# Experts in fixed order with an overflow loop, their first weights loaded early, and the second block's parameters loaded behind the loop

## The reference

```python
scores = jax.nn.sigmoid((hf @ router_w).astype(jnp.float32))
...
_, idx = lax.top_k(jnp.where(emask, sel, -jnp.inf), TOP_K)      # 6 of 64 experts
wts = wts / jnp.sum(wts, axis=-1, keepdims=True) * ROUTED_SCALE
routed = routed_experts(hf, idx, wts.astype(h.dtype), w_gate, w_up, w_down)
shared = swiglu(hf, sw_gate, sw_up, sw_down)
return (routed + shared).reshape(B, T, D)
```

## Time and profile before

| | us |
|---|---|
| median of 3 runs (lowest, highest) | 1790.48 (1787.78, 1791.04) |
| the profiled execution | 1788.62 |
| its span in the trace | 1786.8 |
| PE busy | 1494.7 (84%) |
| DVE busy | 671.1 (38%) |
| ACT busy | 363.8 (20%) |
| DMA moved | 345.25 MB, 193 GB/s mean |

### The profile page before, as it was taken

How to read it: one execution, slowest core, us unless ns; L and a number is a source line. 1 busy time by engine, 2 the same in 40 slices (tenths; PEclk the granted TensorE clock), 3 DMA queues, 4 the chain that set the end, 5 groups by cost and what they waited for, 6 DMA issues and landing times.

```text
span 1786.8 us, 18426 instructions
## 1 busy us (share of the span) xinstructions
PE 1494.7 (84%) x6948; PEld 918.7 (51%) x6948; DVE 671.1 (38%) x1200; ACT 363.8 (20%) x612; POOL 34.4 (2%) x20
## 2 busy tenths in 40 slices
PE   5884974789987899999999999569978777589996
PEld 2342441666754444444444444256656435389974
DVE  1101437533446322222222222353255523366752
ACT  0010212000001122122222222124331111244442
POOL 0000032000000000000000000000000000000000
PEclk9797985899987899999999999769958886789998
DMA  7543160022204699999999999554220221135541
GB/s 275 176 151 108 66 191 0 1 95 95 95 9 166 246 405 401 403 404 401 419 407 408 408 410 404 129 146 148 86 84 1 94 94 48 47 123 176 174 165 71
DMA packets 107278, 345.25 MB, mean 193 GB/s; under 512 B 12551, under 2 KB 38570, under 8 KB 80732
## 3 DMA queue, kind: packets, MB, share of 16 engines
q1 hardware_dynamic: 94072, 325.38, 47.7%
q10 hardware_dynamic: 8500, 15.72, 3.3%
q0 software_dynamic: 4656, 3.44, 0.8%
HBM read 339.50 MB, written 1.05 MB: 191 GB/s over the span
## 4 chain that ended last, share of the span: by engine, by line
PE 60%; DMA 13%; DVE 13%; another core or an unknown queue 4%; issue 3%; SPq 2%; ACT 2%; POOL 1%; ACTq 1%; DVEq 0%; PEldq 0%; POOLq 0%
PE bank L1136 12%; DMA gu_odd<-in_exp_w_up 9%; PE bank L1508 9%; PE bank L1155 5%; PE bank L1157 5%; PE bank L1156 5%; PE bank L1167 2%; PE bank L1528 2%; PE bank L1321 2%; PE bank L1465 2%; PE bank L1580 1%; DMA ring<-in_ada_b 1%; PE bank L1466 1%; PE bank L1483 1%
## 5 line engine op out<-in xcount | busy, mean ns | idle before, releaser
L1136 PE MATMUL bank<-ring,xT 128*128 128x512 f32 (+3 forms) x480 | 199.9, 572 | 18.5 <-DMA ring<-in_w_in 12.9
L1136 PEld LDWEIGHTS bank<-ring,xT 128*128 128x128 f32 x480 | 93.1, 210 | 116.2 <-issue 94.3
L1528 PE MATMUL bank<-dn,tmp 128*64 128x512 f32 x544 | 124.2, 598 | 0.0
L1155 PE MATMUL bank<-mod,w_high 128*128 128x256 f32 x352 | 101.6, 289 | 11.4 <-DVE xT L2680 5.3
L2346 DVE TENSOR_TENSOR xT<-bank,mod 128x512 fp32r<-128x512 f32 x68 | 47.0, 692 | 159.9 <-ACT mod L941 159.9
L1136 PE MATMUL bank<-ring,silu_c 128*128 128x512 f32 x192 | 91.9, 623 | 18.2 <-DMA ring<-in_ada_b 17.7
L2335 DVE SCALAR_TENSOR_TENSOR tmp<-silu_c,rc,bank 128x256 f32<-128x256 f32 x34 | 23.3, 686 | 213.7 <-ACT silu_c L928 213.7
L1156 PE MATMUL bank<-xT,w_high 128*128 128x256 f32 x352 | 99.9, 284 | 0.0
L1157 PE MATMUL bank<-mod,ring 128*128 128x256 f32 x352 | 99.5, 283 | 0.0
L1167 PE MATMUL bank<-c_ident,xn 128*128 128x128 f32 x120 | 27.7, 409 | 76.0 <-DVEq L2370 50.3
L2669 DVE TENSOR_TENSOR ring<-ring,w_high 128x1024 fp32r<-128x1024 f32 x66 | 77.6, 1220 | 26.6 <-ACT w_high L1078 24.6
(11 more groups left out here) (557 smaller groups left out, 2496.6 us busy)
## 6 DMA issues: line engine op xcount, KB each, us to landing
dn<-in_exp_w_down SPq DMA_DIRECT2D x68, 1024.0 KB, 8.0
ring<-in_exp_w_gate SPq DMA_DIRECT2D x34, 1024.0 KB, 9.9
ring<-in_exp_w_up SPq DMA_DIRECT2D x34, 1024.0 KB, 12.0
gu_odd<-in_exp_w_gate SPq DMA_DIRECT2D x34, 1024.0 KB, 11.4
gu_odd<-in_exp_w_up SPq DMA_DIRECT2D x34, 1024.0 KB, 13.4
ring<-in_ada_w SPq DMA_DIRECT2D x12, 2048.0 KB
ring<-in_w_ffn_in SPq DMA_DIRECT2D x22, 1024.0 KB, 5.1
ring<-in_w_in SPq DMA_DIRECT2D x7, 2048.0 KB
```

The lines of the kernel that those rows point to most:

```text
L1136: mm = pe.matmul(bank[lin_bank(o)][:, 0:n], lhs(k, t), ring[:, j % RING, k * n:(k + 1) * n], start=(k == 0), stop=(k == kt - 1 and not bias))
L1155: pe.matmul(out, w[0], x[0], start=start, stop=False, skip_group_check=True)
L1528: mm = pe.matmul(bank[6 + h][CHUNKS[c], :], act_eT[:, 0, k, CHUNKS[c]], dn[:, 2 * parity + c, lo:lo + BANK], start=(k == 0), stop=(k == D_ ...
```

## The change

The loop over all 64 experts has a fixed length of 16 quads with one chunk of up to 64 tokens for each expert, in their order. What an expert has beyond 64 goes to overflow chunks, numbered from 64 on, in a second loop of pairs (`tail`, at least one) on every engine, with the even buffers only and with its own gather of 32 matmuls of 128 columns in place of 16 of 256.

The router's tables move to the unused rows of `gains2`, the shared expert's weights to `sh_w`, a buffer that overlaps `rows2`, `rel` and the second block's constants. SP can then load the shared expert and experts 2 and 3 at `y_ready`, when DVE has finished the mixer, and experts 0 and 1 when `ring` is free. In the loop SP reads no registers from SBUF, and a `dn` buffer is loaded again after its down products (`down_mm`).

The 19 parameter loads move on ACT's queue from before the shared expert to behind the loop. The bias row on PE and DVE and the four hankel copies on ACT move to behind the input projection. DVE waits for the first two gains alone (`first_gains`) before the final norm.

```diff
-MAX_CHUNKS = (T * P * TOP_K + EXPERTS * (CS - 1)) // CS
-MAX_QUADS = -(-MAX_CHUNKS // 4)
-NC = 4 * MAX_QUADS + 8
+QUADS = EXPERTS // 4
+PAIRS = 2 * QUADS
+MAX_OVER = T * P * TOP_K // (CS + 1)
+MAX_TAIL = -(-MAX_OVER // 2)
+NC = EXPERTS + 2 * MAX_TAIL + 4
...
+            sh_w = sb("sh_w", [P, KT * 2 * D_E + (D_E // P) * D], shared)
...
-            sp.wait_ge(mixer_read, 1)
-            gate_up(gu_odd[:, 0, :], A["sh_w_gate"], A["sh_w_up"], sh_full)
-            down(dn[:, 2, :], A["sh_w_down"], sh_full)
-            sp.wait_ge(quads_ready, 1)
-            sp.wait_ge(w_used, J_IN2)
-            quads = sp.value_load(quads_i[0:1, 0:1], min_val=1, max_val=MAX_QUADS)
-            with sp.Fori(0, quads) as i:
+            sp.wait_ge(y_ready, 1)
+            gate_up(sh_gu, A["sh_w_gate"], A["sh_w_up"], sh_full)
+            down(sh_dn, A["sh_w_down"], sh_full)
+            def experts_of_pair(parity, e, gu_free, dn_free):
+                gu_free()
+                for c in range(2):
+                    gate_up(ring[:, c, 0:GU_W] if parity == 0 else gu_odd[:, c, :],
+                            A["exp_w_gate"][e[c]], A["exp_w_up"][e[c]], gu_full[parity])
+                dn_free()
+                for c in range(2):
+                    down(dn[:, 2 * parity + c, :], A["exp_w_down"][e[c]], dn_full[parity])
+            def nothing():
+                pass
+            experts_of_pair(1, (2, 3), nothing, nothing)
+            experts_of_pair(0, (0, 1), lambda: sp.wait_ge(w_used, J_IN2), nothing)
+            with sp.Fori(0, QUADS - 1) as i:
                 for parity in range(2):
                     p = i * 2 + parity
-                    e = [sp.value_load(expert_of[0:1, bass.ds(i * 4 + 2 * parity + c, 1)], min_val=0,
-                                       max_val=EXPERTS - 1) for c in range(2)]
-                    sp.wait_ge(gu_mm, p + 1)
-                    for c in range(2):
-                        gate_up(ring[:, c, 0:GU_W] if parity == 0 else gu_odd[:, c, :],
-                                A["exp_w_gate"][e[c]], A["exp_w_up"][e[c]], gu_full[parity])
-                    sp.wait_ge(spread_mm, p + 2)
-                    for c in range(2):
-                        down(dn[:, 2 * parity + c, :], A["exp_w_down"][e[c]], dn_full[parity])
+                    experts_of_pair(parity, [i * 4 + (4 + 2 * parity + c) for c in range(2)],
+                                    lambda: sp.wait_ge(gu_mm, p + 3), lambda: sp.wait_ge(down_mm, p * 2 + 2))
+            sp.wait_ge(tables_ready, 1)
+            tail = sp.value_load(tail_i[0:1, 0:1], min_val=1, max_val=MAX_TAIL)
+            with sp.Fori(0, tail) as j:
+                e = [sp.value_load(expert_of[0:1, bass.ds(j * 2 + (EXPERTS + c), 1)], min_val=0, max_val=EXPERTS - 1)
+                     for c in range(2)]
+                experts_of_pair(0, e, lambda: sp.wait_ge(gu_mm, j * 2 + (PAIRS + 1)),
+                                lambda: sp.wait_ge(down_mm, j * 2 + 2 * PAIRS))
...
-                act.dma_start(gain_of(i), bcast(A[GAINS[i]])).then_inc(p2_loaded, 16)
+                act.dma_start(gain_of(i), bcast(A[GAINS[i]])).then_inc(first_gains, 16)
...
-            for i, name in enumerate(GAINS):
-                if 2 <= i < len(GAINS) - N_LATE:
-                    act.dma_start(gain_of(i), bcast(A[name])).then_inc(p2_loaded, 16)
-            for i, name in enumerate(ROWS):
-                act.dma_start(rows2[:, i, :], bcast(A[name])).then_inc(p2_loaded, 16)
-            for i in range(3):
-                act.dma_start(rows2[:, 3 + i, :], bcast(A["sconv_w_2"][i])).then_inc(p2_loaded, 16)
-            act.dma_start(conv_w[:, :, :], A["ffn_conv_w_2"]).then_inc(p2_loaded, 16)
-            act.dma_start(conv_b[:, :], A["ffn_conv_b_2"]).then_inc(p2_loaded, 16)
-            act.wait_ge(rel_made, 1)
-            act.dma_start(rel[0:BUCKETS, :], A["rel_bias_2"]).then_inc(p2_loaded, 16)
-            for name in CONST_2:
-                act.dma_start(cst[name][:, :], consts[name]).then_inc(p2_loaded, 16)
...
             act.sem_inc(experts_copied, 1)
-            act.wait_ge(hankel_made, 1)
-            for h in range(GH):
-                row = rel_row[h:h + 1, :]
-                act.dma_start(hankel[:, h, :], bass.AP(row.tensor, row.offset, [list(row.ap[0]), [1, P], [1, 2 * P]]))\
-                    .then_inc(rel_copied, 16)
+            for i, name in enumerate(GAINS):
+                if 2 <= i < len(GAINS) - N_LATE:
+                    act.dma_start(gain_of(i), bcast(A[name])).then_inc(p2_loaded, 16)
...
+            for name in CONST_2:
+                act.dma_start(cst[name][:, :], consts[name]).then_inc(p2_loaded, 16)
...
+            act.wait_ge(hankel_made, 1)
+            for h in range(GH):
+                row = rel_row[h:h + 1, :]
+                act.dma_start(hankel[:, h, :], bass.AP(row.tensor, row.offset, [list(row.ap[0]), [1, P], [1, 2 * P]]))\
+                    .then_inc(rel_copied, 16)
...
+            tail = pe.value_load(tail_i[0:1, 0:1], min_val=1, max_val=MAX_TAIL)
+            with pe.Fori(0, tail) as j:
+                p = j + PAIRS
+                pe.wait_ge(gather_copied, j * 2 + (2 * PAIRS + 4))
+                pe.wait_ge(act_made, p + 2)
+                pe.wait_ge(gu_full[0], j * 64 + (QUADS + 1) * 64)
+                gate_up_products(lambda c: ring[:, c, 0:GU_W], 0).then_inc(gu_mm, 2)
+                pe.wait_ge(pick_ready, j * 2 + (2 * QUADS + 6))
+                pe.wait_ge(y_split, p * 2 + 4)
+                for k in range(KT):
+                    out_k = bank[6 + k // 4][:, k % 4 * P:(k % 4 + 1) * P]
+                    for t in range(T):
+                        pe.matmul(out_k, xn_high[:, t, k * P:(k + 1) * P], pick[:, t, 0:P], start=(t == 0), stop=False)
+                        mm = pe.matmul(out_k, xn_low[:, t, k * P:(k + 1) * P], pick[:, t, 0:P], start=False,
+                                       stop=(t == T - 1))
+                    if k % 4 == 3:
+                        mm.then_inc(gather_mm, 1)
+                pe.wait_ge(put_copied, p + 1)
+                pe.wait_ge(act_made, p + 3)
...
+                put_transpose(p + 1, 0)
+            spread(tail + PAIRS, 1, last=True).then_inc(experts_added, 1)
...
-            pe.wait_ge(p2_loaded, 16 * N_P2)
-            pe.wait_ge(router_sig, 1)
-            pe.wait_ge(x2_ready, 1)
-            pe.matmul(bank[2][0:GH, 0:3 * P], rel[:, :], cst["bucket"][:, :], start=True, stop=True).then_inc(rel_mm, 1)
...
+            pe.wait_ge(p2_loaded, 16 * N_P2)
+            pe.matmul(bank[2][0:GH, 0:3 * P], rel[:, :], cst["bucket"][:, :], start=True, stop=True).then_inc(rel_mm, 1)
...
-            mine, minus = of_chunk[:, 0, :], of_chunk[:, 1, :]
-            link(dve.tensor_scalar(mine, chunk_no[0:EXPERTS, :], rc[0:EXPERTS, 1:2], None, ALU.is_ge))
-            link(dve.scalar_tensor_tensor(mine, chunk_no[0:EXPERTS, :], rc[0:EXPERTS, 2:3], mine, ALU.is_lt, ALU.mult))
-            link(dve.scalar_tensor_tensor(minus, chunk_no[0:EXPERTS, :], rc[0:EXPERTS, 1:2], mine, ALU.subtract,
-                                          ALU.mult))
-            link(dve.tensor_scalar(minus, minus, -float(CS), None, ALU.mult))
+            mine, minus = of_chunk[:, 0, EXPERTS:NC], of_chunk[:, 1, EXPERTS:NC]
+            over_no = chunk_no[0:EXPERTS, EXPERTS:NC]
+            link(dve.tensor_copy(of_chunk[:, 0, 0:EXPERTS], cst["ident"][0:EXPERTS, 0:EXPERTS]))
+            link(dve.memset(of_chunk[:, 1, 0:EXPERTS], 0.0))
+            link(dve.tensor_scalar(mine, over_no, rc[0:EXPERTS, 1:2], None, ALU.is_ge))
+            link(dve.scalar_tensor_tensor(mine, over_no, rc[0:EXPERTS, 2:3], mine, ALU.is_lt, ALU.mult))
+            link(dve.tensor_scalar(minus, over_no, rc[0:EXPERTS, 1:2], 1.0, ALU.subtract, ALU.add))
+            link(dve.scalar_tensor_tensor(minus, minus, -float(CS), mine, ALU.mult, ALU.mult))
...
+                dve.tensor_copy(putT[:, 1, :, :], putT[:, 0, :, :]).then_inc(put_moved, 1)
+                dve.wait_ge(put_moved, j + 1)
+                split_put(p + 1, 0)
...
-            dve.wait_ge(rel_mm, 1)
-            link(dve.tensor_copy(rel_row[:, :], bank[2][0:GH, 0:3 * P]))
-            dve.sem_inc(hankel_made, 1)
-            dve.wait_ge(p2_loaded, 16 * N_P2)
+            dve.wait_ge(first_gains, 32)
...
+            dve.wait_ge(rel_mm, 1)
+            link(dve.tensor_copy(rel_row[:, :], bank[2][0:GH, 0:3 * P]))
+            dve.sem_inc(hankel_made, 1)
```

198 lines of the change are left out of this document (132 added, 66 removed).

## The result

| | us |
|---|---|
| before, median of 4 (lowest, highest) | 1790.76 (1787.78, 1792.5) |
| after, median of 4 (lowest, highest) | 1749.11 (1746.81, 1751.06) |
| ratio, 95% interval | 0.9769 (0.9751 to 0.9786) |
| after, profiled execution; its span | 1751.06; 1749.2 |
| forecast; range | 1763; 1752 to 1781 |

A forecast was written before the change was run, and what follows sets the result against it. The prediction took PE (15.13 us a pair) and DMA (15.50 at 406 GB/s) both to be near their limit in the experts' loop. −20.6 − 14 + 7.3 = −27.3 us gave 1763 us as a median, range 1752 to 1781.

The forecast's parts named there:

- the hankel copies behind the input projection: Projection's end: four issues at the old 8.57 us and a bias row delay `m_exp`, +7.3 us (0.7 to 15.9).
- the bias row and its copy: Projection's end: a short fp32 product on PE ahead of the heads' work, +0.7 us.
- The loop: Experts' loop: one pair less, −15.45 us, and the remaining 32 at 15.13 instead of 15.45, −10.2; together −25.7.
- a last wait: End of the experts' loop: the tail pair waits for the last expert's weights, +1 us (0 to 4).
- the tail's +3.6: Tail pair: register reads +1, gather of 32 products +2, last transposed `put` copy +0.6 us.
- the register reads: Ahead of the tail pair on PE and SP: between 0 and 1.9 us, taken as +1.
- The last `putT`: End of the tail: one transposed `put` copy with no next pair to hide it, +0.6 us (0 to 1.2).
- Behind the loop: Gap up to PE's transposes: shorter without hankel copies, 19 parameter loads against it, −14 us (−17.0 to −4.7).
- the clock: PE's clock behind the gap: less idle might change its level; taken as 0, with −5 us in the range.
- DMA did not pace the loop: Rival, experts' loop: DMA still paces it, gain −14.6 instead of −20.6 us, 1769 as a median; chance 0.15.
- ACT's queue did not stall in the gap: Rival: ACT's queue stalls, −4.7 behind the loop and +15.9 at the projection's end, 1781 as a median; chance 0.15.
- the overflow loop ran once: Rival, overflow loop: it runs twice because more than two chunks overflow, +18 us, 1781; chance 0.03.

The follow-up runs named there:

- Experiments 8: Changed kernel, with SP holding `w_ck` and `w_cv` back until the four hankel copies have landed: 1754.43 us, median of two.
- 12: Kernel before, with ACT's six loads (`mem`, late gains) ahead of the four hankel copies and the first `squares`: 1780.57 us against 1787.07, ratio 0.996.
- Experiments 2: Changed kernel, with the loads of experts 0 to 3 waiting for the router's tables, 0 and 1 first: 1750.75 us.
- 3: Changed kernel, with `dn` buffers in the loop loaded again only after the next pair's spread, as before: 1760.7 us.
- 5: Kernel before, with down weights loaded once the down products' results two pairs earlier are copied: 1781.13 us against 1789.68, ratio 0.9949.
- experiment 1: Kernel before, with only the bias row, its copy and the four hankel copies moved behind the input projection: 1773.57 us against 1789.78, ratio 0.9905.
- the changed kernel's repetition: The changed kernel run again unaltered, five runs: 1752.01 us.
- experiment 9: Kernel before, with both the hankel chain moved behind the input projection and down weights loaded when copied results free them: 1763.5 us, ratio 0.986.
- the improved one: Changed kernel, with hankel copies on SP behind `w_ck` and `w_cv`, and the last 4 of 19 parameter loads behind the second `squares`: 1749.56 us.

## Why the prediction was wrong

The direction and both places were right, the size was not: −27.8 forecast, −39.0 measured in the stretch, and the 4-run median lay another 2.7 us further, of which no trace shows the cause.

- **Mis-sized most: "the hankel copies behind the input projection", +7.3.** Measured +1.60, of which 0.8 is the bias row and its copy (forecast 0.7) and the issues are at most 0.8, where 6.6 was forecast. The step took 8.57 us for four issues from the row of before, as if that were a property of the instructions. Experiments 8 and 12 show that it is one of the moment: the same four issues at the same place took 3.10 us behind `w_ck` and `w_cv` and 8.57 without them, and 8.57 against 2.58 behind the loop. I had put both ends in the bounds, and in choosing I looked at ACT alone; that SP issues 4 MB 1.5 us earlier was to be read from its timeline, and I counted it as a risk.
- **"The loop", −25.7, right in size and wrong in its reason.** The size came out for a reason that I did not have, and in that it was luck. One pair less and 32 waits of 0.32 us came out as computed (33 x 15.45 − 32 x 15.13 = 25.7). But I gave the second part to supply, "4 of 66 experts' weights are out of the loop's DMA load", with the engines at their limit. Experiments 2, 3 and 5 show that the early weights bring nothing and that the condition for `dn` brings all: −10.2 by itself in the kernel before (−10.6 in the loop). In the changed kernel 7.3 us come back in its 32 pairs without it, and 10.8 with the register reads besides. I had noted that `dn` is freed earlier and let it pass as something that doesn't slow SP.
- **"+1" for a last wait, and the tail's +3.6.** The wait isn't there (0). From the 33rd group to ACT's last copy it is 17.14 us, where the last pair before took 15.46: +1.68. Of it 1.6 is the gather:

```profile
1103.71 0.33 PE L1593 MATMUL bank<-mod,gains 128*128 128x128 f32 x1
...
1107.33 0.41 PE L1544 MATMUL bank<-c_ident,tmp 128*128 128x128 f32 x2
```

  3.62 us for 32 products of 128 columns, 0.113 each, against 0.125 for each of the 16 with 256. That halving the columns saves almost nothing was the upper bound's reasoning; the figure of the Trainium skill's page "TensorE: Matmul & The Clock Gate" in the section on the back-to-back issue gap, 81 ns, is under what this trace has. That leaves 0.1 for the register reads, where 1 was forecast. The last `putT` is not in the loop but in the next stretch, at 0.3 us (forecast 0.6).
- **"Behind the loop", −14.** Measured −15.24, made of −17.3 for the hankel chain (experiment 1) and +2.06: 1.1 for the 19 loads, 0.3 for the last `putT`, 0.8 for the clock, which fell sooner, and −0.1 elsewhere. The −17.0 that I had worked out for a quiet queue was the right figure for the first; the loads cost 1.1 us against that kernel, and not the 3 I allowed.
- **Nothing for the clock, the projection and what follows.** −0.9 and −0.4 were measured. The first goes with the clock, which rose 20.2 us behind the transposes' start where it had taken 22.0; in the changed kernel's repetition it is 20.1. I had taken 0 for it, with −5 in the range. The −0.4 is as large as the difference of the two traces of the changed kernel.
- **The range.** Its lower end took all of the loop's and the gap's gain but kept +7.3 for the hankel copies, although I had written down 0.7 as the lower bound of that term. With 0.7 the lower end comes to 1748.5 us, and the measured 1749.11 lies inside.

Of the rivals none happened. DMA did not pace the loop, ACT's queue did not stall in the gap (0.62 us an issue), and the overflow loop ran once.

The whole change as the experiments and the traces divide it, in the stretch: hankel chain −15.4, condition for `dn` −10.2, one pair less −15.1, dearer tail pair +1.7, the early weights 0; sum −39.0. The moved parameter loads, which make room for the buffer that the early loads of the shared expert use, cost 1.1 us, and the later `x2_ready` 1.1 more. The sum closes only because some 2 us are won against the traces of the first and fifth experiments: 1.1 in the projection, where the clock rises sooner, and 1.3 behind `m_exp`, which isn't explained, less 0.4 in the loop and ahead of `m_exp`. One pair less and the tail pair are read from the distances in the traces; no experiment has them alone. (With the first two alone, experiment 9 has two thirds of the gain.)

**Still open:** why four issues of a copy out of one partition are cheap right behind bulk loads of another queue or of ACT's own, and why on SP, behind 4 MB in its own queue, the first of them took 3.82 us and the rest 0.59 to 0.61. Whether an issue stalls while an earlier copy is being carried out, or something in the queue is shared, the runs don't tell apart.

## What to carry to other kernels

A DMA rate that equals the bytes that the loop asks for divided by its period says nothing about a limit, even with the engines' share at 0.99; look at when each load is issued and at what stands ahead of it in its queue's program. A wait on an in-order issuing engine is paid by the loads behind it: put the condition for a buffer as early as the buffer is really free, one line that here gave 10 us. And before a measured issue time is carried to another place, look at what the DMA engines do at both.

## What I had not expected of the hardware

- Four SBUF to SBUF copies of 128 KB, each out of one partition, took 2.58 to 3.10 us of ACT's time to issue in eight of the profiles, 8.56 or 8.57 in three and 13.70 in one; of SP's time 5.75 and 5.98. During the issues the engines moved 372, 293 and 281 GB/s where they took 2.58, 2.87 and 3.10 us, 23 in the kernel before and in the eighth experiment, 139 in the dearest, from loads at its start, and 324 on SP. The median landing on ACT's queue was 13.8 or 13.9 us after issue where the issues were dear, and 14.1 to 17.5 where they were cheap.
- Loads of 512 KB issued behind such copies took 3.28 and 4.96 us, without them 0.36 and 0.45.
- TensorE's clock rose 21.5 to 22.5 us behind the transposes in the kernel before and its variants, and 19.9 to 20.4 in the changed one and all of its variants but the improved one (17.9). In three profiles it stood at the higher level for 3.4 us in between. The projection, from the transposes to `z`'s last copy, took 119.6 us at most and 116.5 in the improved kernel.
- The loop's loads ran at 422 GB/s for 468 us, where 406 had looked like a ceiling.
